# Split-weight slots staggered by 64 bytes modulo 512, and a scratch zone that is no longer rounded to their offset

## What is computed

```python
def swiglu(h, wg, wu, wd):            # h 512 x 1024, wg and wu 1024 x 2816, wd 2816 x 1024
    return (jax.nn.silu(h @ wg) * (h @ wu)) @ wd

for l in range(DEPTH):                # DEPTH = 2
    x = x + 0.5 * swiglu(rms_norm(x, ...), ...)
    x = x + token_mixer(rms_norm(x, ...), w_in[l], ..., w_out[l], ...)
    x = x + 0.5 * swiglu(rms_norm(x, ...), ...)
```

## Time and profile before

| | before |
|---|---|
| median of two runs | 3776.39 us |
| span of the profiled execution | 3773.9 us |
| TensorE matmul busy | 3591.6 us, 95% |
| TensorE weight loads busy | 2848.7 us, 75% |
| VectorE busy | 1361.0 us, 36% |
| ScalarE busy | 1280.9 us, 34% |
| GpSimd busy | 1416.5 us, 38% |
| DMA queue of the loads, share of 16 engines | 29.1% |
| mean granted TensorE clock | 0.973 of 2.4 GHz |

### The profile page before, as it was taken

One profiled execution on the slowest core, in us unless ns is written; L12 is line 12 of the kernel. 1 busy time (PEld: TensorE's weight loads), 2 busy tenths in 40 slices (PEclk: granted clock), 3 DMA queues, 4 the chain that ended last, 5 costly groups with the idle time before them and its releaser, 6 DMA issues. The chain is left out here.

```text
span 3773.9 us, 50732 instructions
## 1 busy us (share of the span) xinstructions
PE 3591.6 (95%) x18352; PEld 2848.7 (75%) x18352; DVE 1361.0 (36%) x1928; ACT 1280.9 (34%) x2014; POOL 1416.5 (38%) x756
## 2 busy tenths in 40 slices
PE   7999999999999999999999998999998997879998
PEld 6888776688887888666688886888886874648886
DVE  4233645542325223645542336111115104561112
ACT  4222435542224223435542224212123234243223
POOL 4444333344444444333344442223232430024443
PEclk8999999999999999999999999999998998889999
DMA  4332443233323333333233332222212321013331
GB/s 133 96 99 84 99 119 113 85 90 98 97 84 101 96 99 89 100 113 107 85 95 100 95 99 63 64 64 61 66 52 61 89 77 52 1 45 93 96 95 61
DMA packets 569026, 322.34 MB, mean 85 GB/s; under 512 B 30266, under 2 KB 563360, under 8 KB 568480
## 3 DMA queue, kind: packets, MB, share of 16 engines
q1 hardware_dynamic: 568864, 320.22, 29.1%
HBM read 318.08 MB, written 2.10 MB: 85 GB/s over the span
## 5 line engine op out<-in xcount | busy, mean ns | idle before, releaser
L874 POOL TENSOR_TENSOR w_lo<-w_raw,w_hi 128x1024 fp32r<-128x1024 f32 x516 | 1273.5, 2468 | 2109.4 <-ACT w_hi L919 2109.4
L919 ACT ACTIVATE w_hi<-w_raw 128x1024 fp32r<-128x1024 f32 x516 | 546.8, 1060 | 1800.7 <-PE psum L2163 1685.8
L2163 PE MATMUL psum<-xg_hi,w_hi 128*128 128x512 f32 x1456 | 572.7, 393 | 12.2 <-DVE xg_lo L1485 10.4
L2163 PE MATMUL psum<-xg_hi,w_lo 128*128 128x512 f32 x1456 | 568.2, 390 | 0.0
L2163 PE MATMUL psum<-xg_lo,w_hi 128*128 128x512 f32 x1408 | 549.5, 390 | 0.0
L2163 PE MATMUL psum<-h_hi,w_hi 128*128 128x512 f32 x1248 | 504.3, 404 | 30.7 <-DVE h_ctx_lo L1534 21.6
L2163 PE MATMUL psum<-h_lo,w_hi 128*128 128x512 f32 x1248 | 491.1, 394 | 0.0
L2163 PE MATMUL psum<-h_hi,w_lo 128*128 128x512 f32 x1248 | 491.1, 393 | 0.0
L2163 PE MATMUL psum<-a_hi,w_hi 128*128 128x512 f32 x1232 | 433.0, 375 | 4.9 <-DVE a_lo L1602 4.2
L2163 PE MATMUL psum<-a_lo,w_hi 128*128 128x512 f32 x1232 | 432.7, 374 | 0.0
L2163 PE MATMUL psum<-a_hi,w_lo 128*128 128x512 f32 x1232 | 432.3, 374 | 0.0
(11 more groups left out here) (454 smaller groups left out, 4399.7 us busy)
## 6 DMA issues: line engine op xcount, KB each, us to landing
w_raw<-ffn_w SPq DMA_DIRECT2D x120, 512.0 KB, 3.8
w_raw<-ffn_w_gate SPq DMA_DIRECT2D x88, 512.0 KB, 3.8
w_raw<-ffn_w_up SPq DMA_DIRECT2D x88, 512.0 KB, 3.8
ada_raw<-ada_w SPq DMA_DIRECT2D x72, 512.0 KB, 4.5
w_raw<-ffn_w_down SPq DMA_DIRECT2D x64, 512.0 KB, 4.1
w_raw<-w_in SPq DMA_DIRECT2D x60, 512.0 KB, 3.8
w_raw<-ffn_w_down SPq DMA_DIRECT2D x32, 384.0 KB, 3.4
w_raw<-w_out SPq DMA_DIRECT2D x24, 512.0 KB, 4.0
```

The source lines that it names most:

```text
L874: nc.gpsimd.tensor_tensor(w_lo[:, i, :], w_raw[:, i, :], w_hi[:, i, :].bitcast(F32), ALU.subtract).then_inc(lo_ready, 1)
L919: nc.scalar.activation(w_hi[:, pos, :], w_raw[:, pos, :], ACT.Copy).then_inc(hi_ready, 1)
L2163: last = nc.tensor.matmul(dst, w[:, pos, k * P:(k + 1) * P], rhs[g][r](k0 + k), start=k == 0 and m == 0, stop=k == nk - 1 and m == 2)
```

## The change

Every slot of w_hi and w_lo gets 16 more float32 (64 bytes) behind it that nobody uses, so that slot i lies 64i bytes past a multiple of 512 from the array's start. Each array grows by 256 bytes, so w_lo begins 256 bytes further modulo 512, and h_hi is at the old offset again. The rounding ahead of the zone is taken out. The tiles between h_hi and the zone have lengths that add up to 288 modulo 512, so this is where the zone now begins.

Start modulo 512 bytes, counted from the offset of x_lat, w_raw and h_hi:

| tile | before | after |
|---|---|---|
| w_raw, h_hi, h_lo, squares, normed, rstd | 0 | 0 |
| w_hi, slot i | 0 | 64i |
| w_lo, slot i | 0 | 256 + 64i |
| zone: a, a1, xg, mix_lo, h_ctx, silu, gated | 0 | 288 |
| latents, latents_hi, latents_lo | 128 | 416 |

```diff
 SLOTS = 4
 SLOT = KD * P
+W_PAD = 16
...
         w_raw = put("w_raw", [P, SLOTS, SLOT])
-        w_hi = put("w_hi", [P, SLOTS, SLOT], F32R)
-        w_lo = put("w_lo", [P, SLOTS, SLOT], F32R)
+        w_hi = put("w_hi", [P, SLOTS, SLOT + W_PAD], F32R)[:, :, 0:SLOT]
+        w_lo = put("w_lo", [P, SLOTS, SLOT + W_PAD], F32R)[:, :, 0:SLOT]
         h_at = top[0]
...
         decay = put("decay", [P, 2, RET_H])
-        top[0] = h_at + (top[0] - h_at + 511) // 512 * 512
         zone = top[0]
```

## The result

The changed kernel takes 3836.98 us (two runs, 3831.59 and 3842.36), the kernel before 3776.39: a ratio of 1.0163, 95% interval 1.0146 to 1.018. The change costs some 60 us. That is within the 2% band and within the prediction's whole range (3690 to 3880), but outside the 3765 to 3795 of the forecast's own case. It is also three times what executions of one kernel differ by: 13 runs of the kernel before, in one round of the experiments, lay between 3765.66 and 3786.11 us.

A forecast was written before the change was run, and what follows sets the result against it. TensorE, busy 95% of the span, was taken as the bound, mostly through line 2163's matmul beat. The profiled span of 3773.9 us plus 0, with the runs' median 2.5 us over it, gave 3776; range 3690 to 3880.

The forecast's parts named there:

- the forecast's own case: Whole kernel: the address change costs 0, time 3776 us, own range 3765 to 3795, chance 0.53.
- Part 1 and 2: Line 2163: staggered weight slots and the zone at 288 together cost 0 per matmul.
- the good latent item: Latents' matmuls (line 2361), item at 531.19: 227.5 ns each, read as the steady beat at another distance.
- Each distance is met once in every load.: Line 2163: the stream gains 512 bytes on each 128-column weight load, whatever the starting distance; reason for cost 0.
- The slow latent item: Latents' matmuls (line 2361), item at 526.71: 232.5 ns each; as upper bound everywhere, 6.0 ns a matmul, +77 us.
- +44 us: Upper bound: the slower pace of FFN1's last part in block 2 at every line 2163 matmul, 3.4 ns each.
- The +24 us for a beat found anew at every slot: Line 2163: each 24-matmul slot spends some eight beats searching, at 5.5 ns each; an in-between price.
- the 13 ns: Line 2163 at full clock: surplus of each load and matmul pair beyond its 512 columns' 213.3 ns.
- C: Line 2163: the surplus beyond the columns goes, so faster; half case 3702 us; chance 0.15, 0.12 beyond 2%.
- Parts 3 and 4: Other engines and the rest of the zone: TensorE doesn't feel ScalarE or GpSimd, other distances stay; cost 0.
- rival D: Making of w_lo slows on GpSimd, so TensorE idles before line 2163: 310 us, 4086; chance 0.02.
- B: Line 2163: changing distances lose the locked beat, 229 to 240 ns; +24 to +77 us, middle 3826; chance 0.30.

The follow-up runs named there:

- e4: Changed kernel with w_hi and w_lo slots both at 64i, the zone at 256 and h at 0: 3822.11 us, 1.0119 of the kernel before.
- e1: Changed kernel with only the zone's rounding removed: zone rows at 288, h and all weight slots at 0; 3821.21 us, 1.0114 of the kernel before.
- e3: Changed kernel's layout with only w_lo 256 bytes further, slots not staggered and the zone level: 3777.05 us, 1.0005 of the kernel before.
- e11: Kernel before, with dense (line 2163) multiplying only the upper 16 bits of each float32, read as bf16 at the same addresses: 3749.96 us, one run.
- e6: Changed kernel's layout with only w_lo moved, by 64 bytes; w_hi and all rows at 0: 3824.32 us, 1.0127 of the kernel before.
- e5: Changed kernel's layout with all distances 0 and everything from x_lat on 32 bytes further: 3769.5 us, 0.9986 of the kernel before.
- e2: Changed kernel with only the weight slots staggered and the zone at 0: 3824.96 us, 1.0125 of the kernel before.
- e8: Changed kernel with w_hi and w_lo slots 48 bytes apart, the zone at 160 and h at 0: 3823.58 us in one run.
- e10: The changed kernel once more, with no edit, for a second profile: 3841.62 us.
- e9: The kernel before once more, with no edit, for a second profile: 3777.23 us.

## Why the prediction was wrong

*What bounds the kernel.* Right: TensorE's beat in line 2163, and nothing else, carried the change. Right too that a beat must be read from starts. In h the mean duration moved by 3 ns (404 to 407), while slot 1 slowed by 6.2 and slot 0 hardly at all.

*Part 1 and 2, "The value taken: 0".* This step failed: the price per matmul of line 2163 was put at 0, and the runs showed +6.6 ns on xg and a, and +3.3 on h (the mean of its four slots, 230.5 against 227.2), in all some 60 us. That is also over the 2 ns a family that the prediction had named as the sign of being wrong. The value rested on two reasons, and both fell.

- *"Another distance brought no beat under 226 ns there", from the good latent item.* I read this item as a row at distance 128. But its chunks of 96 columns lie at 0, 128, 256 and 384 with the rows at 128, and modulo 256 every second one is at distance 0. It was a mixture, and of the two items with that mixture I took the better as the state and the worse (232.5 ns) as an accident. A steady distance of 128 gives 232.1 in e4. Of two rows that differ at one layout, neither shows alone what the layout costs.
- *"Each distance is met once in every load."* From 0.84 ns a column I worked out that load and stream slide past each other by a whole period, so that the starting distance drops out. e1 and e4 refute the conclusion: there nothing but the starting distance changes, and the beat changes with it. That a load's recorded duration tells the pace at which it reads SBUF was assumed, not shown.

*Period.* "Multiples of 512 are alike" was right; e3 and e4 show that 256 counts as 0 too. With a period of 256 the step between w_hi and w_lo is harmless, and 64i and 288 are the whole of the change. The prediction had left the divisors open.

*The bounds.* The slow latent item everywhere (6.0 ns, +77 us) was the right size for xg and a (6.6), and too much for h, whose slot 0 stays at distance 0. With the earlier trace rows's +44 us as the other upper bound the truth, +61, lay between. The +24 us for a beat found anew at every slot isn't what happened: the slow slots are slow from end to end (5.60 us are 24 matmuls of 233.3 ns). A faster beat was out of reach: distance 0 is the best of those measured, and e11 shows that 12 of the 13 ns stay even with a load half as long. The range reaches down to 3690 because of C, the rival in which the surplus goes, whose half case is 3702, 74 us below 3776. No run shows that term: it is half of 148 us, 11.5 ns for each of the 12,864 matmuls, an estimate of mine from half of the 430 ns between the loads of the earlier trace rows. In its place the runs showed 226.7 ns as the lowest mean at any distance for the float32r matmul (F32R in the diff) of 512 columns, and 225.0 in the fastest slots with 16-bit operands.

*Parts 3 and 4.* Right: GpSimd and ScalarE keep their durations, TensorE never waits for w_lo, and rival D has no idle time to show.

*The rivals.* B was the one that came true, 11 us over the middle of its price (3837 against 3826) and with part of its mark: slots and families differ. The other part did not show. w_hi and w_lo differ by under 1 ns, and two slots of h, at 227.7 and 228.9 ns, stay under the 229 to 240 it gave. Its mechanism was partly wrong: it laid the cost to the change of distance at every second or third matmul and at every slot. e3, with the change of 256 bytes only, costs nothing, and e1, with one fixed distance of 288 for all, costs 43 us. A change of 64 bytes does cost more than its share (e6). What the prediction had for it, the slow latent item at another distance, was the right sign; that the total also fell near B's middle is luck, since the price came from other states than those measured. The 13 ns beyond the columns were no sign of it: they are there at distance 0, and e11 shows that some 12 of them stay with a load half as long. C fell: no mean of the sixteen distances is under 226.7 ns.

*Beside other engines, and between load and stream.* The prediction had the beat the same with and without GpSimd beside it, and that stands: in the kernel before, the starts with xg and a are 226.7 ns apart while GpSimd is at work and 226.8 while it rests, in the changed one 233.5 and 233.3. Between the two operands of TensorE it is otherwise. For 32-bit operands at full clock their start addresses move the beat from 226.7 to 234.4 ns, while moving both alike does nothing (e5, 226.7 to 227.5). With 16-bit operands the effect is nearly gone (225.4 to 226.7).

## What to carry to other kernels

Where every float32r matmul of 512 columns has its own weight load, keep the starts of the moving and of the stationary operand equal modulo 256 bytes, through every slot and chunk, and round a scratch region to that offset even when nothing seems to need it: in this kernel a matmul then takes 226.7 ns, against up to 234.4 at fifteen other distances, and that is worth 43 to 61 us in 3776. A pad between buffers can cost time even though no instruction changes (47 us in e2). To see such a cost, count matmuls in a stretch in which TensorE never rests, or take starts slot by slot; busy share (95% in both kernels) and mean duration (393 and 399 ns for xg) hide it, and a row that mixes two distances tells neither.

## What the runs showed that I had not expected

- The beat isn't monotonic in distance: 233.3 ns at 8 bytes, 227.5 to 228.3 at 16, 231.1 at 24, 233.3 at 32, 228.9 at 64. Distances of opposite sign differ (8 and -8: 233.3 and 230.7; 64 and -64: 228.9 and 233.3). No mechanism is shown for this order.
- At one distance a slot can keep one of two paces: 226.7 or 228.3 ns at 16 bytes (e8), 228.9 or about 232.5 at 64 (e10), 225.0 or 226.7 at 0 with 16-bit operands (e11). What picks it wasn't found.
- Some 12 ns beyond the columns remain with equal offsets and with loads half as long (e11). What they are stays open.
- Alternating streams of 512 and 256 columns run at 347 or 353 ns a pair with one layout and one program, in two executions (before and e9) and, by the earlier trace rows, even within one. What sets it wasn't found.
- 256 bytes count as 0 (226.7 to 226.9 ns with xg and a in e3) and 128 don't (232.1 ns), so the period is 256 for chunks like these. Whether chunks that don't step by whole multiples of 256 follow the same table wasn't tried.
